# Start of a two-block transformer kernel: TensorE multiplies zeros while x loads, and the first weight piece is multiplied in three steps

## The reference, cut to what matters

```
h = rmsnorm(x, norm_mix_g)      # x * rsqrt(mean(x*x) + 1e-6) * g
u = h @ w_in                    # 1024 -> 5376 columns
```

## Time and profile before

| What | Value |
|---|---|
| median of 3 runs | 1466.34 us (1465.89 to 1468.03) |
| the profiled execution | 1466.11 us |
| its span in the trace | 1464.3 us |
| mean granted TensorE clock | 0.998 |
| TensorE busy | 1438.5 us (98%) |
| VectorE busy | 1012.6 us (69%) |
| ScalarE busy | 767.6 us (52%) |
| GpSimd busy | 29.4 us (2%) |
| read from memory | 246.59 MB, 169 GB/s over the span |

### The profile page before, as it was taken

One profiled execution on the slowest core, in us unless ns is written; L12 is line 12 of the kernel. 1 busy time (PEld: TensorE's weight loads), 2 busy tenths in 40 slices (PEclk: granted clock), 3 DMA queues, 4 the chain that ended last, 5 costly groups with the idle time before them and its releaser, 6 DMA issues.

```text
span 1464.3 us, 22900 instructions
## 1 busy us (share of the span) xinstructions
PE 1438.5 (98%) x9382; PEld 1233.8 (84%) x9382; DVE 1012.6 (69%) x1340; ACT 767.6 (52%) x1045; POOL 29.4 (2%) x96
## 2 busy tenths in 40 slices
PE   7999999999999999999999999999999999999999
PEld 7999998888887788888878888888888887788887
DVE  5785667787447787647776877468774688687753
ACT  6744464655335565435675555355553456565542
POOL 0000000000001200000000000000000000000000
PEclk9999999999999999999999999999999999999999
DMA  8441125555554465554424555545555454255552
GB/s 327 145 173 60 60 87 188 203 203 192 186 201 144 147 227 186 188 201 165 155 84 148 202 197 179 196 166 207 182 192 200 145 178 145 83 203 198 179 196 86
DMA packets 35959, 249.11 MB, mean 170 GB/s; under 512 B 4112, under 2 KB 4240, under 8 KB 6416
## 3 DMA queue, kind: packets, MB, share of 16 engines
q1 hardware_dynamic: 35568, 247.52, 47.6%
q10 hardware_dynamic: 288, 0.13, 0.0%
HBM read 246.59 MB, written 1.05 MB: 169 GB/s over the span
## 4 chain that ended last, share of the span: by engine, by line
PE 64%; ACT 2%; DVE 1%; issue 1%; POOL 0%; DVEq 0%; ACTq 0%; POOLq 0%
PE ps L1852 19%; PE ps L1806 9%; PE ps L1851 9%; PE ps L1808 9%; PE ps L1807 9%; PE ps L1848 3%; PE ps L1849 1%; PE ps L2155 1%; PE ps L2135 1%; PE ps L1881 1%; PE ps L2144 0%; DVE lo L2512 0%; ACT hi L2186 0%; PE ps L2084 0%; DVE X L2565 0%
## 5 line engine op out<-in xcount | busy, mean ns | idle before, releaser
L2512 DVE TENSOR_TENSOR lo<-raw,hi 128x2048 fp32r<-128x2048 f32 (+1 forms) x230 | 525.2, 2285 | 235.3 <-ACT hi L2186 234.8
L2186 ACT CAST hi<-raw 128x2048 fp32r<-128x2048 f32 (+1 forms) x230 | 438.3, 1907 | 239.5 <-PE ps L1808 235.7
L1852 PE MATMUL ps<-h,hi 128*128 128x512 f32 x1456 | 519.2, 396 | 0.0
L1851 PE MATMUL ps<-h,lo 128*128 128x256 f32 x1456 | 406.7, 279 | 0.8 <-DVE h L2540 0.8
L1852 PEld LDWEIGHTS ps<-h,hi 128*128 128x128 f32 x1456 | 273.3, 188 | 56.0
L1851 PEld LDWEIGHTS ps<-h,lo 128*128 128x128 f32 x1456 | 274.5, 189 | 10.6 <-DVE h L2540 1.1
L1806 PE MATMUL ps<-hi,a 128*128 128x512 f32 x584 | 230.3, 394 | 0.0
L1808 PE MATMUL ps<-hi,a 128*128 128x512 f32 x584 | 227.6, 390 | 0.0
L1807 PE MATMUL ps<-lo,a 128*128 128x512 f32 x584 | 227.4, 389 | 0.0
L2375 ACT COPY a<-ps 128x256 f32<-128x256 f32 x208 | 76.1, 371 | 204.5 <-PE ps L1852 199.2
L1806 PEld LDWEIGHTS ps<-hi,a 128*128 128x128 f32 x584 | 109.6, 188 | 24.0 <-issue 2.2
(11 more groups left out here) (330 smaller groups left out, 1592.3 us busy)
## 6 DMA issues: line engine op xcount, KB each, us to landing
raw<-ws SPq DMA_DIRECT2D x229, 1024.0 KB, 4.8
X<-xin SPq DMA_DIRECT2D x8, 256.0 KB, 5.4
const<-const SPq DMA_DIRECT2D x1, 1352.0 KB, 11.9
raw<-ws SPq DMA_DIRECT2D x2, 512.0 KB, 6.7
out<-X SPq DMA_DIRECT2D x4, 256.0 KB, 2.1
small<-small SPq DMA_DIRECT2D x1, 992.5 KB, 13.8
a<-row SPq DMA_DIRECT2D x1, 512.0 KB, 5.9
a<-pin SPq DMA_DIRECT2D x1, 256.0 KB, 5.1
```

Source lines behind the costliest of these rows:

```text
L1851: e.matmul(b2(sl)[:, 0, :], wl[:, k, a:a + 128], HH[:, k, :], start=False, stop=False)
L1852: t = e.matmul(b2(sl), wh[:, k, a:a + 128], h2[:, k, :, :], start=False, stop=k == 7)
L2186: e.copy(hi[j % NSPL][:, n], raw[j % NRAW][:, n]).then_inc(hi_ready, 1)
L2512: e.tensor_tensor(lo[j % NSPL][:, n], raw[j % NRAW][:, n], hi[j % NSPL][:, n].bitcast(F), ALU.subtract).then_inc(lo_ready, 1)
```

## The change

TensorE, before its first transposes, multiplies zeros into the bank of the first part: eight matmuls of 128 x 512, on a strip of `lo[2]` that VectorE has set to zero; then it waits for the identity only (`ident_in`), and the wait for `cols` moves to VectorE. ScalarE issues the identity ahead of `cols`. Ahead of the first products TensorE multiplies the identity by itself nine times. In the hand-written order, both right-half parts of x come ahead of `hi` 0, and both of their low parts ahead of `first_lo` and `lo` 0. The products of piece 0 are made in three steps: high weights by both parts of h for k = 0 to 3, the same for k = 4 to 7, and all products with the low weights last. Everything behind piece 0 is as before, `n_rows` directly behind it too.

```
@@ program: semaphores and buffers @@
         first_in = sem("first_in")
+        ident_in = sem("ident_in")
+        zeroed = sem("zeroed")
...
+        zeros = lo[NSPL - 1][:, 0:512]
@@ the script @@
+        def first_piece(c, needs, evac):
+
+            piece_check("w_in", 0, 0, c)
+            yield from split(0)
+            yield from room(1)
+            sl = take()
+            for part in range(3):
+                cur[0] = max(cur[0], lo_due[0] if part == 2 else h_due[1, part])
+                emit("first", pe=16 * 0.12, part=part, slot=sl, need=unmet(needs(4 * min(part, 1))))
+                if part < 2:
+                    yield "pe"
+            piece_done(0, sl)
+            if not evac(sl, c, NSPL):
+                give(sl)
+            yield "pe"
...
         nm.low(0, 0)
         nm.low(1, 0)
         emit("first_hi")
-        emit_hi(0)
-        emit("first_lo")
         nm.part(0, 1)
         nm.part(1, 1)
-        emit_lo(0)
+        emit_hi(0)
         nm.low(0, 1)
         nm.low(1, 1)
+        emit("first_lo")
+        emit_lo(0)
         emit_hi(1)
         nm.stat(0, 0)
...
-                yield from cols_piece("w_in", 0, c, "h", nm.h_needs, shift)
+                if p == 0:
+                    yield from first_piece(c, nm.h_needs, shift)
+                else:
+                    yield from cols_piece("w_in", 0, c, "h", nm.h_needs, shift)
@@ tensor_program @@
+            def warm(sl, n, w, x):
+
+                for _ in range(n):
+                    e.matmul(banks[sl.b][:, 0:x.shape[1]], w, x, start=True, stop=True)
...
+                if kind == "first":
+                    part = s["part"]
+                    wh = hi[0][:, :].rearrange("p (k n) -> p k n", k=8)
+                    wl = lo[0][:, :].rearrange("p (k n) -> p k n", k=8)
+                    if part == 0:
+                        claim(sl)
+                        warm(sl, 9, ident, ident)
+                        e.wait_ge(first_hi, 1)
+                    elif part == 1:
+                        e.wait_ge(hi_ready, 1)
+                    if s["need"]:
+                        e.wait_ge(s["need"][0], s["need"][1])
+                    if part < 2:
+                        for u in range(2):
+                            for k in range(4 * part, 4 * part + 4):
+                                w = wh[:, k, 128 * u:128 * u + 128]
+                                e.matmul(b2(sl)[:, u, :], w, HH[:, k, :], start=(u, k) == (0, 0), stop=False)
+                                e.matmul(b2(sl)[:, u, :], w, HL[:, k, :], start=False, stop=False)
+                    else:
+                        e.wait_ge(first_lo, 1)
+                        for u in range(2):
+                            for k in range(4):
+                                e.matmul(b2(sl)[:, u, :], wl[:, k, 128 * u:128 * u + 128], HH[:, k, :], start=False, stop=False)
+                        e.wait_ge(lo_ready, 1)
+                        for u in range(2):
+                            for k in range(4, 8):
+                                t = e.matmul(b2(sl)[:, u, :], wl[:, k, 128 * u:128 * u + 128], HH[:, k, :], start=False,
+                                             stop=(u, k) == (1, 7))
+                        t.then_inc(full[sl.b], 1)
+                elif kind == "cols":
...
                 elif kind == "n_part":
                     claim(sl)
-                    e.wait_ge(first_in, 32)
+                    if s["n"] == 1:
+                        e.wait_ge(zeroed, 1)
+                        warm(sl, 8, zeros[:, 0:128], zeros)
+                        e.wait_ge(ident_in, 16)
                     e.wait_ge(s["x"][0], s["x"][1])
@@ scalar_program @@
+            e.dma_start(ident, constin[:, 0:128]).then_inc(ident_in, 16)
             e.dma_start(cols[:, :], colsin).then_inc(first_in, 16)
-            e.dma_start(ident, constin[:, 0:128]).then_inc(first_in, 16)
@@ vector_program @@
+            e.memset(zeros.bitcast(F), 0.0).then_inc(zeroed, 1)
             for s in script:
...
+                    if n == 1:
+                        e.wait_ge(first_in, 16)
                     ready(sl)
...
-                    e.wait_ge(first_in, 32)
+                    e.wait_ge(first_in, 16)
```

More of the change, by code:

```diff
@@ L1812, in tensor_program @@
                 sl = s.get("slot")
-                if kind == "cols":
+                if kind == "first":
[28 more added lines that the diff above has]
+                elif kind == "cols":
                     j = s["i"] % NSPL
@@ L1819, in tensor_program @@
                     if s["opens"]:
[L1820 to L1823, removed]
+                        e.wait_ge(lo_ready, s["i"] + 1)
                         claim(sl)
-                    if (s["i"], s["o"], s["k0"]) == (0, 0, nk // 2):
-                        e.wait_ge(lo_ready, 1)
                     if s["need"]:
```

## The result

The changed kernel takes **1469.61 us** (median of 12, 1468.49 to 1471.48), the kernel before 1466.24 us (12 runs): ratio **1.0024** with a 95% interval of 1.0016 to 1.0032, 3.4 us slower. The forecast was 1467.8 and the range ended at 1469.6, a hundredth of a us under the median. The profiled execution took 1471.08 us with a span of 1469.3.

What follows compares the result with a forecast made beforehand. PE was taken to bound the kernel, with `n_rows` held by the root: -0.3 us from the root plus 1.75 from the low clock gave +1.4, forecast 1467.8 us, range 1465.3 to 1469.6.

Steps and rivals of the forecast that it cites:

- the root holds PE: Behind piece 0: `n_rows` waits some 4 to 5 us for DVE's second diagonal, so a faster piece 0 alone gains nothing.
- the root itself gains 0.3: Start of `hi` 1 to `n_rows`: chain stays 8.22 us but starts at piece 1's landing, 12.6 instead of 12.95.
- 18 matmuls at 0.217 instead of 0.12, 18 x 0.097 = 1.75 us: Start of `n_rows` and piece 1: low clock after PE's 4.9 us idle time costs 1.75 us, bounds 0 to 3.0.
- -0.3 + 1.75 = +1.45: Whole start: root's gain of 0.3 us and low clock's price of 1.75, summed to +1.4 us in the prediction.
- the rival in which the clock holds: Gap behind piece 0: identity and closer products carry the full clock over it, leaving -0.3 alone, 1466.0 us; chance 0.15.
- The prediction's estimate from the Trainium skill: Piece 1's start: cold matmuls vary between runs, costing 1.2 to 2.7 us in place of 1.75; sums 1467.2 to 1468.7.
- the rest is unchanged: From piece 1 on: PE's order of work stays the same, the planner's share is nothing.
- it is covered: Start of DVE: the memset of the zeros, taken as 0.6 us, ends before DVE's first work at 6.59.
- cost nothing: Start of PE: eight zero matmuls, 1.9 to 3.5 us, fit in PE's idle time until 5.43.
- no cost to the end either way: Ahead of piece 0: nine identity products, 2.0 to 4 us, fill PE's wait before `first_hi`.
- the wait at 226 us: PE's later wait of 1.7 us, among its longest after 60 us, so piece 1's loss reaches the end nearly whole.
- the one in which the low clock lasts: `n_rows` and all of piece 1: low clock for 6.8 us, +2.7 us net, 1469.0; chance 0.16.

Runs made afterwards that it cites:

- e15: The changed kernel run again unchanged, for a second trace: 1469.43 us, ratio 1.0019.
- e3: The changed kernel with `n_rows` moved on PE from behind piece 0 to behind piece 1: 1467.92 us, ratio 1.0011.
- e1: The kernel before run again unchanged, for a second trace and the scatter: 1466.42 us, ratio 1.0000.
- e6: The kernel before plus zeros, identity ahead of `cols` and nine identity products, with old start order and old piece 0: 1468.90 us, ratio 1.0012.
- e9: The kernel before with only the memset of the zeros on VectorE added: 1467.38 us, ratio 1.0003.
- e10: The kernel before with 13 identity products (52 instructions) on PE ahead of piece 0: 1468.13 us, ratio 1.0003.
- e14: The kernel before with the VectorE memset and a wait for `first_in` ahead of VectorE's first multiply: 1467.00 us, ratio 1.0009.
- e2: The changed kernel with 20 identity matmuls filling PE's gap between piece 0 and `n_rows`: 1467.68 us, ratio 1.0011.
- e5: The changed kernel without zeros, memset and identities, so new order and three-step piece 0 alone: 1467.88 us, ratio 1.0008.
- e7: The changed kernel with the gap ahead of `n_rows` filled by identity matmuls and the memset on GpSimd: 1465.63 us, ratio 0.9996.
- e11: The changed kernel with the memset moved to GpSimd and nothing else changed: 1469.65 us, ratio 1.0016.
- e16: The kernel before with `n_rows` behind piece 1 and piece 2 loaded ahead of the constants: 1465.69 us, ratio 0.9994.
- e13: Changed kernel without zeros, memset, identities; `n_rows` behind piece 1, piece 2 loaded ahead of constants, 226 us wait filled: 1463.46 us, ratio 0.9980.
- e8: Changed kernel with `n_rows` behind piece 1, piece 2 loaded ahead of constants, memset on GpSimd, 226 us wait filled: 1464.12 us, ratio 0.9984.

## Why the prediction was wrong, point by point

**Right: the root holds PE.** `n_rows` waited 4.52 us (4.83 in e15) for the second diagonal where I said 4 to 5, piece 0 ended at 15.8 for 16.0, and e3 showed piece 1 at 16.7 as soon as the root was out of the way.

**Right: the root itself gains 0.3.** The chain of 8.22 us that I read off the trace before is 8.21 to 8.26 us, from the start of `hi` 1 to `n_rows`, in all twelve traces in which `n_rows` stands behind piece 0. What scatters is when `hi` 1 starts, and so `n_rows`: at 21.17, 20.76, 20.97, 20.83, 21.07 and 20.88 in the old order (before, e1, e6, e9, e10, e14), 20.95 in the mean, and at 20.32, 20.83, 20.50, 20.58, 20.40 and 21.04 in the new (after, e2, e5, e7, e11, e15), 20.61. One trace against one would not have shown it.

**Right in kind, short in size: the clock.** The step "18 matmuls at 0.217 instead of 0.12, 18 x 0.097 = 1.75 us" is the first that failed. It is 2.75 us in the changed kernel's first trace and 2.1 to 2.65 in the three others with the long wait (e15, e5, e11). The low clock lasted 6.1 us after work resumed at 20.32, and 4.7 in e15, not the 4.0 of the one event in the trace before. I took that row as the price because it was the same kind of event, and left the whole low stretch of the same trace, 6.8 us, to a bound and a rival; the stretch was 6.8 us long again in all four traces, and began 0.7 to 2.1 us ahead of `n_rows`, so 4.7 to 6.1 us of it fell on work. At the start as a whole, root and clock together, the first trace holds -0.85 + 2.75 = +1.9 us and e15 -0.13 + 2.1 = +2.0, for the forecast -0.3 + 1.75 = +1.45. So this step was short by about half a us. All 23 executions of the changed kernel (after and e15) have a mean clock under 1.0, and all four traces with the long wait show the low clock behind it: the rival in which the clock holds was never seen. (A mean under 1.0 doesn't say where the clock was low, so for the executions without a trace this is argued.)

The prediction's estimate from the Trainium skill ("TensorE: Matmul & The Clock Gate", Part 1), that one kernel shows different numbers of cold matmuls, reached to 2.7 us. The traces agree with that page in kind: 6.1 and 4.7 us of matmuls at the low clock in two executions of one kernel.

**Wrong: "the rest is unchanged".** The order was the same, as I said. But I took the same order for the same times. The steps that put the memset, the zeros, the nine identities and the moved wait at nothing ("it is covered", "cost nothing", "no cost to the end either way") are the larger failure: in their own place they did cost nothing, and 100 to 500 us later they cost 0.7 us (PE's 52 instructions; e10's trace shows it without the rest) and 0.7 us (e14: the memset and the wait). By the table of lateness, without the second low clock: 1.95 at the start, 0.7 on PE and 0.7 on VectorE, which is 3.35 for the 3.4 of the medians. Of the 1.8 us by which the forecast fell short, this is about 1.4 and the start about 0.5. That the median stands only just past the range, and e15's 1469.43 inside it, is luck: the upper bound was made for a longer low clock at the start, and not for this.

**Wrong as a share of the scatter: the wait at 226 us.** I used its 1.7 us to say that a loss isn't absorbed there. It isn't. But the change makes it 2.05 (e14 shows by what), and behind it the clock is low in some executions: 1.45 us in the profiled one, which is why that one took 1471.08.

Of the rivals, the one in which the low clock lasts came nearest, at 1469.0, and in mechanism too: 6.1 us of its 6.8 fell on work in the first trace. It lacked what wasn't at the start.

## What to carry to other kernels

Before making a stage faster, find what else ends at the same time behind it: here piece 0 and the root ended within 0.02 us of each other, and the gain of 5 us became a wait of 4.5 and a low clock. Price an added instruction where it stands and also as a shift of everything behind it in that engine's stream; it is cheap to look, by setting each instruction's start in one trace against the same instruction's in the other. And keep warming work only where a run without it is slower. All eleven traces with it ahead of piece 0 have the first products at the full clock, and of the seven without it four (before, e5, e14, e16); yet e13, one of the other three, is no slower than e8, because what stands behind piece 0 gave the difference away.

## What the runs showed of the hardware that I had not expected

One instruction more at the head of VectorE's stream costs nothing (e9), that and one wait more cost 0.35 us at 226 us and again at 508 us (e14), each time as a delay ahead of one instruction for which the profile shows no reason. On PE the idle time by no releaser near 107 us is 0 with no instruction added, 0.3 to 0.6 us with 52, 2.6 with 84, and 0 with 132.

The granted clock was low after waits of 1.76 us (e1), 1.86 to 1.88 us (e10, e11 and e13, near 495 us) and 2.05 us (after), and stayed full over a wait of the same length in the same place in other executions (1.76 in e9 and e10, 1.85 in before, 2.05 in e2 and e14); after waits of 4.5 to 4.8 us it was low in every trace (after, e5, e11, e15).

The clock of 1.00 that the view gives at the very start is not to be trusted: in before the transposes took 421 ns each while it read 1.00, and 273 for the last of them, and in e1, e9 and e13 the first products of piece 0 ran 0.21 us apart under it.
